# An expert stage with 80 instead of 96 slots per expert

## What is computed

```python
def _moe_swiglu(u, w_router, w_gate, w_up, w_down):
    xt = u.reshape(n_tok, dm)                                # 256 x 1024
    logits = jnp.dot(xt, w_router).astype(jnp.float32)       # 8 experts
    top_logits, top_idx = lax.top_k(logits, TOP_K)           # TOP_K = 2
    top_w = jax.nn.softmax(top_logits, axis=-1).astype(u.dtype)
    ...
    h = jax.nn.silu(lax.ragged_dot(xs, w_gate, group_sizes)) * lax.ragged_dot(xs, w_up, group_sizes)
    ys = lax.ragged_dot(h, w_down, group_sizes) * top_w.reshape(-1)[order][:, None]
    out = jax.ops.segment_sum(ys, tok, num_segments=n_tok)
```

## Time and profile before

| what | value |
|---|---|
| median of 3 runs | 2401.27 us (2396.63 to 2406.88) |
| profiled execution | 2399.09 us |
| its span in the trace | 2397.3 us |
| granted TensorE clock, mean | 0.934 of full speed |
| TensorE (PE) busy | 2180.4 us, 91% |
| VectorE / ScalarE / GpSimd busy | 694.5 / 141.8 / 160.6 us |
| instructions | 68445 |
| read from memory | 653.9 MB, 273 GB/s over the span |

### The profile page before, as it was taken

How to read it: one execution, slowest core, us unless ns; L and a number is a source line. 1 busy time by engine, 2 the same in 40 slices (tenths; PEclk the granted TensorE clock), 3 DMA queues, 4 the chain that set the end, 5 groups by cost and what they waited for, 6 DMA issues and landing times.

```text
span 2397.3 us, 68445 instructions
## 1 busy us (share of the span) xinstructions
PE 2180.4 (91%) x31915; PEld 1793.0 (75%) x31915; DVE 694.5 (29%) x1496; ACT 141.8 (6%) x270; POOL 160.6 (7%) x196
## 2 busy tenths in 40 slices
PE   5699989999999979988999797599999999999995
PEld 2478777777677768547777574399989989989894
DVE  7765342222222232144324414511010110101014
ACT  1102010000000000001000001100000000000000
POOL 8980000000000000000000000000000000000000
PEclk9899869999999978979999897799999999999997
DMA  9952567999999995316667431279999999989991
GB/s 343 320 184 107 187 234 276 395 395 394 393 393 394 395 376 182 118 53 229 238 225 269 150 123 57 88 263 348 342 342 346 386 334 339 371 303 383 329 340 39
DMA packets 304861, 658.13 MB, mean 275 GB/s; under 512 B 19844, under 2 KB 40852, under 8 KB 304660
## 3 DMA queue, kind: packets, MB, share of 16 engines
q1 hardware_dynamic: 295072, 646.99, 73.6%
q0 software_dynamic: 1456, 5.24, 0.7%
q10 hardware_dynamic: 8132, 2.72, 0.5%
HBM read 653.88 MB, written 1.05 MB: 273 GB/s over the span
## 4 chain that ended last, share of the span: by engine, by line
PE 80%; DMA 8%; DVE 6%; issue 4%; ACT 1%; SPq 1%; DVEq 0%; ACTq 0%
PE ps L1432 78%; DMA ring<-in_w_down_dram 8%; DVE arena L771 2%; PE ps L1440 2%; SPq L320 1%; DMA x<-in_x_dram 0%; ACT hT L543 0%; DVE stat L870 0%; DVE arena L1315 0%; ACTq L494 0%; DVE x L848 0%; DVE x L879 0%; DVE x L850 0%; DVEq L771 0%; DVE tok L796 0%
## 5 line engine op out<-in xcount | busy, mean ns | idle before, releaser
L1432 PE MATMUL ps<-arena,ring 128*64 128x96 f32 (+2 forms) x25216 | 990.7, 239 | 25.4 <-issue 23.3
L1432 PEld LDWEIGHTS ps<-arena,ring 128*64 128x64 f32 (+1 forms) x25216 | 972.0, 138 | 52.3 <-issue 45.3
L1432 PE MATMUL ps<-hT,ring 128*128 128x256 f32 x1616 | 353.1, 381 | 18.0 <-ACT hT L543 18.0
L1432 PEld LDWEIGHTS ps<-hT,ring 128*128 128x128 f32 x1616 | 307.6, 191 | 60.7 <-DVE stat L813 16.3
L1432 PE MATMUL ps<-ring,arena 128*64 128x512 f32 (+1 forms) x880 | 285.6, 616 | 16.9 <-DMA ring<-in_w_down_dram 14.4
L1432 PE MATMUL ps<-arena 128*128 128x128 f32 (+7 forms) x1296 | 244.5, 360 | 28.0 <-DVE arena L1143 11.4
L1168 DVE TENSOR_TENSOR arena<-arena,ps 128x384 f32<-128x384 f32 (+1 forms) x80 | 38.5, 481 | 760.2 <-PE ps L1432 760.2
L1432 PEld LDWEIGHTS ps<-ring,arena 128*64 128x64 f32 (+1 forms) x880 | 109.3, 165 | 175.2 <-issue 171.4
L1432 PEld LDWEIGHTS ps<-arena 128*128 128x128 f32 (+4 forms) x1296 | 167.3, 202 | 84.0 <-issue 52.7
L596 ACT ACTIVATE arena<-ps 128x384 f32<-128x384 f32 (+1 forms) x80 | 34.6, 432 | 1221.5 <-PE ps L1432 1221.5
L487 POOL DMA_DIRECT2D rowB<-in_ln_g_dram x4 | 2.1, 534 | 1357.4 <-DVE stat L1275 1017.4
(11 more groups left out here) (300 smaller groups left out, 859.3 us busy)
## 6 DMA issues: line engine op xcount, KB each, us to landing
ring<-in_moe_w_gate_dram SPq DMA_DIRECT2D x40, 2048.0 KB, 10.1
ring<-in_moe_w_up_dram SPq DMA_DIRECT2D x40, 2048.0 KB, 10.4
ring<-in_moe_w_down_dram SPq DMA_DIRECT2D x40, 2048.0 KB, 9.2
ring<-in_w_gate_dram SPq DMA_DIRECT2D x32, 2048.0 KB, 19.8
ring<-in_w_up_dram SPq DMA_DIRECT2D x32, 2048.0 KB, 19.7
ring<-in_w_down_dram SPq DMA_DIRECT2D x32, 2048.0 KB, 18.9
ring<-in_w_in_dram SPq DMA_DIRECT2D x18, 2048.0 KB, 10.4
ring<-in_w_ada_dram SPq DMA_DIRECT2D x12, 2048.0 KB, 20.9
```

The lines of the kernel that those rows point to most:

```text
L1432: ins = pe.matmul(*args, **kw)
```

## The change

One constant: the large experts have 80 slots instead of 96.

```diff
 SL = 128
-CAP1, CAP2 = 64, 96
+CAP1, CAP2 = 64, 80
 EPG1, EPG2 = SL // CAP1, SL // CAP2
```

## The result

The changed kernel takes 2411.51 us (2401.53 to 2419.74) against 2396.72 us (2382.44 to 2407.02) for the kernel before, measured side by side, 20 executions each: ratio 1.0064, 95% interval [1.0046, 1.0082]. It is slower by 15 us, a small difference but clear of the noise, where 18 us less was forecast.

The account below looks back on a forecast made before the run. PE in the second expert stage, waiting for code: 17 pages x 5.75 us x 8 experts gives 782 against 796.4 us, 14 gained; with 3 at the end, 1 at the start and 0.3 behind, 18 us, so 2383; range 2316 to 2425.

Parts of the forecast that it names:

- PE waits for its code, a page of 256 instructions at a time: Second expert stage: the equally spaced "issue" holes, 128 records apart, are PE waiting for instruction packets of 16.4 KB.
- A record of 80 columns takes 35.4 ns: Weight products of the second expert stage: 5.9 ns saved on each of 2112, 12.5 us per expert, 100 us offered.
- 17 packets per expert whatever the columns: Second expert stage: an expert is 2162 records, 16.9 pages of code, and narrower products leave that count unchanged.
- The weights don't bind alone: Second expert stage: code was taken as the tighter supply; the rival that weights bind gave 2321 us, chance 0.21.
- floor of 87.8 to 91.8 us per expert: Time to load one expert's 34.6 MB of weights in the second expert stage at 394 to 377 GB/s.
- At the end 3 us, PE's own pace: End of the second expert stage: loads are over, code comes in 3.5 us, so 480 + 64 shorter records gain 3 us.
- The 1 us at the start: Start of the second expert stage: another 1 us gained before the code supply lags.
- The holes: Second expert stage: many more "issue" holes at 128 records' distance, some 110 us in total instead of 22.
- the price of a page: Second expert stage: one page of code comes every 5.75 us, the middle of 5.3 and 6.2; 97.8 us per expert.
- the sign turns at 5.86: Second expert stage: from a mean page of 796.4/136 = 5.86 us upward the change makes the kernel slower.
- hole regime everywhere: Slower rival: every page of the second expert stage, not one in four, takes 6.2 us; 43 us lost, 2444; chance 0.15.
- only the end moves: Rival: the 6.0 us average between packets is already all supply; only 4 us of start and end gained, 2397; chance 0.14.

Follow-up runs that it names:

- the loop: Changed kernel (80 slots) with each expert's four middle pieces as a hardware loop of two passes over two pieces on PE: 2343.19 us, ratio 0.9793 to the kernel before.
- the quarter: Changed kernel (80 slots) with 16 tiny products before the first expert, moving page borders by a quarter of a load: 2380.46 us, ratio 0.9957 to the kernel before.

## Why the prediction was wrong

By its own steps:

- *PE waits for its code, a page of 256 instructions at a time.* Right, and now shown: the holes looked at end 1.2 to 1.4 us behind a packet of code, fewer pages with the same work remove holes (52 instead of 95), and a quarter of the bytes of weights with the same pages removes them all. 32 inserted products count as 128 instructions, 64 of them product records, so the 128 records of a page are 256. That PE's entering a page asks for the next one stood in a rival without a row for it; in the changed kernel the packet starts 3.8 us after PE enters a page (1804.21 and 1808.0, 1810.47 and 1814.2, 1816.74 and 1820.5).
- *A record of 80 columns takes 35.4 ns.* It takes 34.7 where no page is late (the kernel with a quarter of each load), so 80 columns offer 6.6 ns a record, 13.9 us per expert, a little more than the 12.5 forecast. Right. The changed kernel's busy time fell by only 89 us, because a row behind a hole lasts longer (36.3 ns a record).
- *17 packets per expert whatever the columns.* 101 packets in the six experts from 1673 to 2290, as there were 101 in six of the kernel before. Right.
- *The weights don't bind alone.* Right: 340 GB/s in the stage, below the 377 of the earlier trace rows, and no wait on a load among the holes. Its floor of 87.8 to 91.8 us per expert was never reached with whole loads: the nearest is 92.3, with the loop at 375 GB/s, and PE waits for no load there either.
- *At the end 3 us, PE's own pace.* 480 records took 2378.41 - 2361.47 = 16.9 us against 2357.97 - 2338.02 = 20.0 in the earlier trace rows, at a DMA share of 0.14. Right. The 1 us at the start was not there: the first expert took 102.4 us against 96.6, the supply was late at once.
- *The holes.* Some 110 us forecast, 125 to 128 measured. Right in kind, short by 15 to 18.
- **The step that failed is the price of a page, "I take the middle, 5.75".** Measured over the whole stage it is 815.9/136 = 6.00 us. The prediction had worked out that the sign turns at 5.86; 0.25 us per page times 136 is 34 us, which is the whole miss of 18 + 15. The mechanism was right, and this term of its sum, 17 x 5.75 = 97.8 us per expert, was too small: 102.0 was measured. The forecast case and the "hole regime everywhere" rival (6.2, 2444 us) lay 0.45 us apart, and what came is between them, past the turning point.

Why the middle was a bad choice can be said from the rows that it rested on. The lower bound, 5.3 us, came from the expert without holes. There a page was asked for every 5.3 us, so the row shows that pages can come in 5.3 us at that moment, not that they would keep doing so. With 64, 80 and 88 columns the interval that repeats is 6.2 to 6.3 us, which is the value of the earlier trace rows, a stretch in which PE truly waited. A stretch in which the engine waits shows the supply; one in which it doesn't shows at most a bound on it. But the waiting stretch alone would not have given the time either: 6.2 us for every page is the 2444 us of the slower rival, too high by 33; about a third of the pages are not late even in the changed kernel. That loads stand in the DMA engines ahead of each page's code, by which that rival gets there, no run shows: with transfers of a quarter of the size the interval is 6.26 us as before. The "only the end moves" rival rested on the right row, 605 us/101 = 6.0 us per packet, and was set aside because PE asks for little between experts. The changed kernel has 100 packets in the same window of 605 us: the pace stayed, as that rival says. It was nearest to what happened, and it had 0.14; its 2397 us is still 15 too low.

Beyond that, the rows of before give no hold on the sign. With 80 columns three places of the page borders span 2380 to 2412 us, which is more than the forecast gain, and with the quarter a page costs 97.0/17 = 5.71 us and the kernel takes 2380, all but the 5.75 and 2383 of the forecast: another place of the borders would have made it look right by luck. What the mechanism supports is "no change", give or take 0.7%. The range, 2316 to 2425, held the time because it reached halfway to the slower rival.

What stays open: why a page takes 5.2 us at one time and 6.26 or 6.86 at another, and by what way the place of the borders acts. The mean load of the DMA engines doesn't tell them apart: over 1650 to 2250 the share is 0.98 with 80 columns and the quarter, where an expert takes 97.0 us, and 0.93 unmoved, where it takes 102.0. The size of a transfer is excluded as the cause of the 6.26; the order in which the packets of weights and of code are served was not tried.

## What to carry to other kernels

Before you make an unrolled stream of short products shorter, divide its time by its pages of code: here 128 product records with their weight loads are one page, pages came every 6.0 us on average while weights streamed at 340 GB/s, and records shorter than the 41 ns of 96 columns bought nothing as long as the code stayed as it was. If "issue" holes lie at equal distances of records, shorten the code first (a loop of a few pages gave 2.1%, and only then did fewer columns pay), or move fewer bytes; judge a change of under 1% in such a stage at several places of the page borders. And take the price of a supply from a stretch in which the engine waits for it, not from one in which it doesn't, and ask separately how many of the pages will be late.

## What the runs showed that was not expected

- Inserting 16 or 32 products of one column moves the whole kernel by -1.1% to +0.9%, of which the 7.0 us of the 32 products themselves are at most 0.3%.
- The holes often come in steps of about 0.27 us: page intervals of 5.43, 5.72, 5.98 and 6.26 us with 80 columns (in the rows of the changed kernel above, 1834.41 - 1828.98 is 5.43 and 1828.98 - 1823.00 is 5.98), and 5.21 and 6.86 with the quarter, six steps apart. The kernel with 96 columns and borders moved by half has holes of one to four steps:

```profile
1807.77 10.93 PE L1432 MATMUL ps<-arena,ring 128*64 128x96 f32 x255 [1.09 <-issue]
1819.51 5.50 PE L1432 MATMUL ps<-arena,ring 128*64 128x96 f32 x128 [0.82 <-issue]
1825.28 5.50 PE L1432 MATMUL ps<-arena,ring 128*64 128x96 f32 x127 [0.27 <-issue]
1831.32 5.50 PE L1432 MATMUL ps<-arena,ring 128*64 128x96 f32 x128 [0.54 <-issue]
```

  What takes steps of that length was not shown.
- A hardware loop of six pages on TensorE runs its second pass at full pace, 34.8 ns a record, with no packet on the instruction queue between 1892 and 1918 us.
- Half of the weight traffic (share 0.61) is as good for the code as a quarter (0.34): 4.44 us per page could be met in both, but for 7 holes with half. The delay sets in somewhere between a share of 0.61 and 0.93; nothing in between was run.
